# The first mixer's value, gate and memory-query columns computed token by token, with its heads turned between output units

## The reference

```python
proj = rms_norm(x, mix_norm_g) @ a_w_in       # q, k (4 heads x 128), v, o (4 x 256), gates (8), xq (4 x 128)
h = num / maximum(abs(den), exp(-m_t))        # num = (q k' * decay) v, den = row sums of the weights
h = rms_norm(h, h_norm_g) * sigmoid(o)        # norm over a head's 256 columns
p = softmax(rms_norm(xq, q_norm_g) @ mem_k' * 128 ** -0.5)
x = x + concatenate([h, p @ mem_v]) @ a_w_out
```

## Time and profile before

| | us |
|---|---|
| median of 3 runs | 1548.07 |
| lowest and highest run | 1547.05, 2189.37 |
| the profiled execution, whole | 1546.74 |
| its span, first to last instruction | 1544.8 |
| PE busy | 1534.3 |
| DVE, ACT, POOL busy | 967.8, 813.4, 220.7 |
| mixer A, from its first matmul to its last output unit | about 215 to 345 |

### The profile page before, as it was taken

How to read it: one execution, slowest core, us unless ns; L and a number is a source line. 1 busy time by engine, 2 the same in 40 slices (tenths; PEclk the granted TensorE clock), 3 DMA queues, 4 the chain that set the end, 5 groups by cost and what they waited for, 6 DMA issues and landing times.

```text
span 1544.8 us, 20354 instructions
## 1 busy us (share of the span) xinstructions
PE 1534.3 (99%) x8114; PEld 1312.3 (85%) x8114; DVE 967.8 (63%) x1108; ACT 813.4 (53%) x1003; POOL 220.7 (14%) x220
## 2 busy tenths in 40 slices
PE   9999999999999999999999999999999999999998
PEld 7888888988888888888888888899988899888886
DVE  6655566666555565556776555589998566665555
ACT  7544454565444454445776444466887343454444
POOL 0211100011111021110001211100571000021110
PEclk9999999999999999999999999999999999999999
DMA  7776666445866567656425776656554665557662
GB/s 250 253 218 204 193 190 211 137 155 172 229 209 213 179 204 222 216 182 196 144 75 168 242 210 206 195 189 201 187 180 151 214 191 191 170 180 224 211 216 89
DMA packets 261679, 296.04 MB, mean 192 GB/s; under 512 B 63812, under 2 KB 223840, under 8 KB 261600
## 3 DMA queue, kind: packets, MB, share of 16 engines
q1 hardware_dynamic: 260496, 293.64, 61.0%
q10 hardware_dynamic: 1104, 1.31, 0.2%
HBM read 280.71 MB, written 1.09 MB: 182 GB/s over the span
## 4 chain that ended last, share of the span: by engine, by line
PE 96%; issue 1%; POOL 1%; DMA 0%; DVE 0%; ACT 0%; ACTq 0%; POOLq 0%; DVEq 0%
PE ps L2137 25%; PE ps L2141 25%; PE ps L2138 25%; PE ps L2127 5%; PE ps L2128 4%; PE ps L2129 4%; PE ps L2180 1%; PE ps L2291 1%; DMA scr<-in_mem_dram 0%; PE ps L2422 0%; PE ps L2405 0%; POOL scr L662 0%; PE ps L2700 0%; PE ps L2602 0%; PE ps L2575 0%
## 5 line engine op out<-in xcount | busy, mean ns | idle before, releaser
L1266 DVE TENSOR_TENSOR w_lo<-w_raw,w_hi 128x2048 fp32r<-128x2048 f32 x255 | 591.8, 2323 | 368.0 <-ACT w_hi L719 367.9
L719 ACT ACTIVATE w_hi<-w_raw 128x2048 fp32r<-128x2048 f32 x255 | 487.3, 1913 | 379.8 <-PE ps L2141 332.2
L2137 PE MATMUL ps<-w_hi,xg_hi 128*128 128x512 f32 (+1 forms) x1072 | 417.9, 390 | 0.0
L2141 PE MATMUL ps<-w_hi,xg_lo 128*128 128x512 f32 (+1 forms) x1072 | 415.6, 388 | 0.0
L2138 PE MATMUL ps<-w_lo,xg_hi 128*128 128x512 f32 (+1 forms) x1072 | 415.5, 388 | 0.0
L2137 PE MATMUL ps<-w_hi,y_hi 128*128 128x512 f32 x666 | 261.9, 393 | 0.8 <-DVE w_lo L1285 0.5
L2141 PE MATMUL ps<-w_hi,y_lo 128*128 128x512 f32 x666 | 259.1, 389 | 0.0
L2138 PE MATMUL ps<-w_lo,y_hi 128*128 128x512 f32 x666 | 258.9, 389 | 0.0
L2137 PEld LDWEIGHTS ps<-w_hi,xg_hi 128*128 128x128 f32 x1072 | 201.3, 188 | 41.5 <-issue 0.7
L2141 PEld LDWEIGHTS ps<-w_hi,xg_lo 128*128 128x128 f32 x1072 | 201.3, 188 | 41.4
L2138 PEld LDWEIGHTS ps<-w_lo,xg_hi 128*128 128x128 f32 x1072 | 201.3, 188 | 40.8
(11 more groups left out here) (339 smaller groups left out, 1148.7 us busy)
## 6 DMA issues: line engine op xcount, KB each, us to landing
w_raw<-in_ffn_w_in_dram SPq DMA_DIRECT2D x176, 512.0 KB, 4.8
w_raw<-in_ffn_w_out_dram SPq DMA_DIRECT2D x88, 512.0 KB, 4.4
w_raw<-in_w_in_dram SPq DMA_DIRECT2D x82, 512.0 KB, 4.7
w_raw<-in_a_w_in_dram SPq DMA_DIRECT2D x28, 512.0 KB, 4.6
w_raw<-in_w_gate_dram SPq DMA_DIRECT2D x22, 512.0 KB, 4.0
w_raw<-in_w_up_dram SPq DMA_DIRECT2D x22, 512.0 KB, 5.0
w_raw<-in_w_down_dram SPq DMA_DIRECT2D x22, 512.0 KB, 4.1
w_raw<-in_w_ssd_proj_dram SPq DMA_DIRECT2D x16, 512.0 KB, 4.7
```

The lines of the kernel that those rows point to most:

```text
L719: act.activation(w_hi[:, u % RING, :], w_raw[:, u % RING, :], ACT.Copy).then_inc(w_rounded, 1)
L1266: dve.tensor_tensor(w_lo[:, s, :], w_raw[:, s, :], w_hi[:, s, :].bitcast(F32), ALU.subtract).then_inc(w_split, 1)
L2137: pe.matmul(dst, xh, hi, start=start, stop=False, skip_group_check=True)
L2141: return pe.matmul(dst, xl, hi, start=False, stop=stop, skip_group_check=True)
```

## The change

All units of mixer A from u+5 on become row units, in the order memory query (u+5, u+6), values (u+7 to u+10), output gate (u+11 to u+14). The memory query is turned by 8 transposes on PE (`memory_query_turn`); its squares are summed by DVE instead of PE. `den` becomes a column per token (12 matmuls of one column and two small transposes), and the heads' sum of squares is taken by ACT with an accumulator while it reads the numerator from PSUM. The gated heads lie by token and are turned to channels by PE, 8 transposes at a time (`head_turn`), once between output units v and v+1 and once between v+1 and v+2. ACT's `high_` then reads these turned heads from PSUM. The output units take the memory part first (v, v+1), then the heads (v+2 to v+5). One of two round trips of rows through memory goes away, and so do POOL's four `tensor_scalar` instructions on the gate.

```diff
-    add("mixa", "ggggg" + "dddd" + "g" * 6)
...
+        GA = [4 + (U["mixa"] + k) % RING for k in range(3)]
+        MA = min(GA[2], GA[0])
+        PAIRS = ((GA[1], STAT), (GA[2], GA[0]))
...
+                sp.wait_ge(vec_done, vec.at("A -m"))
+                sp.dma_start(a_spread, a_rows[0:4, GM]).then_inc(a_stored, 16)
+                sp.wait_ge(a_stored, 16)
+                sp.dma_start(a_nm, a_spread.partition_broadcast(P)).then_inc(nm_landed, 16)
                 for j in range(6):
-                    load(U["mixa_out"] + j, d_src(a["a_w_out"][0], 256 * j))
+                    load(u + 9 + j, row_src(w, 512 * (j % 2), D + 512 + 512 * (j // 2)))
+                for j, k in enumerate((4, 5, 0, 1, 2, 3)):
+                    load(U["mixa_out"] + j, d_src(a["a_w_out"][0], 256 * k))
...
+                for tt in range(2):
+                    act.wait_ge(w_used, u + 7)
+                    act.activation(xq_arows[:, tt], ps[:, PAIRS[1][tt], :], ACT.Identity, scale=rcol[:, tt:tt + 1]).then_inc(act_done, act_(f"A xr {tt}"))
+                for tt in range(2):
+                    act.wait_ge(act_done, act_.at(f"A xr {tt}"))
+                    act.activation(xsq_arows[:, tt], xq_arows[:, tt], ACT.Square).then_inc(act_done, act_(f"A xsq {tt}"))
+                round_(u + 9)
+                for j in range(2):
+                    act.wait_ge(pe_done, pe_.at("A xT"))
+                    act.activation(xq_a[:, 2 * j:2 * j + 2], tiles(ps[:, PAIRS[1][j], :]), ACT.Identity,
+                                   scale=gain_qk[:, 0:1]).then_inc(act_done, act_(f"A xq {j}"))
+                root(m_r, m_v, load=False)
+                round_(u + 10)
...
                                        scale=rcol[:, tt:tt + 1]).then_inc(act_done, act_(f"A v {g} {tt}"))
-                round_(u + 8)
-                round_(u + 9)
                 value_columns(0)
-                round_(u + 10)
                 round_(u + 11)
+                mem_exps("A", p_a)
+                round_(u + 12)
                 value_columns(1)
-                round_(u + 12)
-                act.wait_ge(pe_done, pe_.at("A num 3"))
+                round_(u + 13)
+                mem_turned("A", pt_a, 0)
...
-                    act.wait_ge(vec_done, vec.at(f"A h {h}"))
-                    act.activation(a_hsq[:, 2 * h:2 * h + 2], a_h[:, 2 * h:2 * h + 2],
-                                   ACT.Square).then_inc(act_done, act_(f"A hsq {h}"))
-                round_(u + 13)
-                query_squares("A", u + 9, xq_a, xsq_a, 0)
-                root(KB(28, 4), KB(24, 4))
-                round_(u + 14)
-                root(m_r, m_v, load=False)
+                    act.wait_ge(pe_done, pe_.at(f"A num {h}"))
+                    for tt in range(2):
+                        c = 2 * h + tt
+                        act.activation(a_squares[:, c], half(h, tt), ACT.Square, scale=a_rd[:, c:c + 1],
+                                       accum_out=a_sum[:, c:c + 1]).then_inc(act_done, act_(f"A hsq {c}"))
+                root(a_y2, a_v2, load=False)
                 act.preload_act_table_set(SETS["exp"])
-                def tanh(j):
-                    evacuated(u + 11 + j)
-                    act.activation(a_o[:, 2 * j:2 * j + 2], a_o[:, 2 * j:2 * j + 2], ACT.Tanh,
-                                   scale=0.5).then_inc(act_done, act_(f"A tanh {j}"))
-                def high(j):
-                    act.wait_ge(vec_done, vec.at(f"A y {j}"))
-                    act.activation(y_hi[:, 2 * j:2 * j + 2], a_h[:, 2 * j:2 * j + 2], ACT.Copy).then_inc(act_done, act_(f"A hi {j}"))
+                def tanh(g):
+                    for tt in range(2):
...
+                        act.wait_ge(w_used, u + 13 + 2 * g)
+                        act.activation(a_o[:, tt, 512 * g:512 * g + 512], ps[:, PAIRS[g][tt], :], ACT.Tanh,
+                                       scale=r_half[:, tt:tt + 1]).then_inc(act_done, act_(f"A tanh {g} {tt}"))
+                def high_(g):
+                    act.wait_ge(pe_done, pe_.at(f"A yT {g}"))
+                    for k in range(4 * g, 4 * g + 4):
+                        act.activation(y_hi[:, k], half(PAIRS[g][k % 4 // 2], k), ACT.Identity,
+                                       scale=col("h_norm", k)).then_inc(act_done, act_(f"A hi {k}"))
                 tanh(0)
-                round_(u + 15)
-                high(0)
+                round_(v)
+                high_(0)
+                round_(v + 1)
                 tanh(1)
-                mem_exps("A", p_a)
-                high(1)
-                round_(u + 16)
-                tanh(2)
-                high(2)
                 round_(v + 2)
-                tanh(3)
-                mem_turned("A", pt_a, 4)
-                high(3)
-                round_(v + 3)
-                mem_high("A", 4)
-                for j in range(4, 7):
+                high_(1)
+                for j in range(3, 7):
                     round_(v + j)
...
+                for tt in range(2):
+                    dve.wait_ge(act_done, act_.at(f"A xsq {tt}"))
+                    dve.tensor_reduce(xq_sum.rearrange("p (h t) -> p t h", t=2)[:, tt], xsq_arows[:, tt].rearrange("p (h d) -> p h d", d=M_HD),
+                                      AXX, ALU.add).then_inc(vec_done, vec(f"A xsum {tt}"))
...
                 dve.wait_ge(vec_done, vec.at("A den"))
-                dve.reciprocal(g[:, GL], g[:, GL]).then_inc(vec_done, vec("A rden"))
+                dve.reciprocal(a_rd, a_rd).then_inc(vec_done, vec("A rden"))
+                split(u + 9)
...
+                mem_max("A")
                 split(u + 11)
...
                 gated(0)
-                evac(a_o[:, 2:4], u + 12)
-                split(u + 15)
-                low_a(0)
+                split(v)
+                low_(0)
+                split(v + 1)
                 gated(1)
-                mem_probs("A", p_a)
-                low_a(1)
-                evac(a_o[:, 4:6], u + 13)
-                evac(a_o[:, 6:8], u + 14)
-                split(u + 16)
-                gated(2)
-                low_a(2)
                 split(v + 2)
-                gated(3)
-                low_a(3)
-                split(v + 3)
-                mem_low("A", 4)
-                for j in range(4, 7):
+                low_(1)
+                for j in range(3, 7):
                     split(v + j)
...
-            def row_unit(u, banks, X, kt0, start, stop):
+            def row_unit(u, banks, X, kt0, start, stop, between=None):
...
                     tok = slice(tt * P, tt * P + P)
                     for k in range(4):
                         last = row_passes(ps[:, banks[tt], :], X[0][:, kt0 + k, tok], X[1][:, kt0 + k, tok], s, 512 * k, start and k == 0, stop and k == 3)
...
-                def value_unit(j):
+                g = a_rows[0:4]
+                def rows_of(j, banks, **kw):
+                    row_unit(u + j, banks, (xg_hi, xg_lo), 4 * ((j - 5) % 2), j % 2 == 1, j % 2 == 0, **kw)
+                def gate_columns(row, bank_, c0):
+                    for tt in range(2):
+                        last = pe.transpose(ps[:, bank_, c0 + 4 * tt:c0 + 4 * tt + 4], g[:, row, tt * P:tt * P + P], ident[0:4, 0:4])
+                    return last
+                def scores():
+                    evacuated(u + 4)
+                    for h in range(4):
+                        pe.matmul(ps[:, h, 0:T], a_k[:, h, 0:P], a_q[:, h], start=True, stop=True)
+                        pe.matmul(ps[:, h, T:384], a_k[:, h, P:], a_q[:, h, P:], start=True,
+                                  stop=True).then_inc(pe_done, pe_(f"A s {h}"))
+                def blocks(h):
+                    return ((0, a_s[:, h, 0:P], 0, True, True), (1, a_s[:, h, P:T], 0, True, False), (1, a_s[:, h, T:], 1, False, True))
+                def den():
+                    pe.wait_ge(vec_done, vec.at("A s 3"))
+                    for h in range(4):
+                        for tt, weights, _, first, end in blocks(h):
+                            pe.matmul(ps[:, 0, 2 * h + tt:2 * h + tt + 1], weights, ones[:, 0:1], start=first, stop=end, skip_group_check=True)
+                    pe.wait_ge(act_done, act_.at("A em"))
+                    gate_columns(GE, 0, 8).then_inc(pe_done, pe_("A den"))
+                def memory_query_turn():
+                    pe.wait_ge(act_done, act_.at("A xr 1"))
+                    for h in range(4):
+                        for tt in range(2):
+                            last = pe.transpose(half(PAIRS[1][h // 2], h)[:, tt * P:tt * P + P], xq_arows[:, tt, h * P:h * P + P], ident[:, :])
+                    last.then_inc(pe_done, pe_("A xT"))
+                def num():
+                    pe.wait_ge(act_done, act_.at("A v 1 1"))
+                    for h in range(4):
+                        for tt, weights, block_, first, end in blocks(h):
```

(79 more changed lines are left out.)

154 lines of the change are left out of this document (57 added, 97 removed).

## The result

The kernel after takes 1552.92 us (median of six runs, 1552.30 to 1554.12), the kernel before 1546.94 us beside it (median of six). The ratio is 1.0039, with a 95% interval from 1.0029 to 1.0049: slower by 4.5 to 7.6 us, within 2%. The profiled execution of after took 1552.74 us, its span is 1551.0 us.

What follows compares the result with a forecast made beforehand. PE was taken to bound the kernel, its matmuls' pace plus any added wait. Terms -2.4 + 5.9 + 0.45 + 2.3 = +6.2 us on the profiled 1546.7 gave 1552.9, stated as 1553.0 us; range 1549.5 to 1557.0.

Steps and rivals of the forecast that it cites:

- What bounds the kernel: Whole kernel: time is PE's matmuls at their issue pace plus any added wait; savings on DVE, ACT or POOL worth nothing.
- PE's own work: Mixer A: matmuls and transposes removed, added and changed in layout sum to -2.4 us.
- The six units: Mixer A: six units change to row layout, 5.45 us each instead of 5.75, -1.8 us.
- The two groups of sums: Mixer A: the heads' sums (L2473, 1.54 us) and the query's sums (L2398, 1.70 us) on PE both go.
- The 24 transposes: Mixer A: 8 transposes of the query and 16 of the heads are added, +2.5 us.
- The wait at v+1: Output unit v+1: PE idles while ACT rounds turned heads, then v+1, and DVE splits it, 5.9 us.
- The wait at v+3: Output unit v+3, after the second turn: PE needs it 5.45 us later, the chain takes 5.9, +0.45 us.
- The clock behind the wait: Unit v+1: clock falls within the wait, restart at 1.2 GHz, half of a 4.5 to 5 us ramp lost, +2.3 us.
- Its two ends: Clock evidence from the kernel's ends: 4.5 to 5 us at half pace at the start, fall from 4.1 us of idleness on.
- The rival in which the clock holds: Output units: the clock stays full through the single wait, giving 1550.7 us; chance 22%.
- The rival with a slow unit v+1 throughout: Mixer A: longer ramp or a second late unit, 3 us more than forecast, 1556 us; chance 17%.
- The rival on the other side: Unit v+1: rounding and split done when `head_turn(0)` ends, wait hidden, only PE's saving left, 1544.3 us; chance 4%.

Runs made afterwards that it cites:

- the spread kernel: Kernel after with head halves one output unit later in ACT's and DVE's lists and `den`'s matmuls spread through unit u+8: 1543.84 us, ratio 0.998 to the kernel before.
- the run with both orders: Kernel after with rounding and split of v+1 and v+3 moved ahead of the heads' steps on ACT and DVE: 1545.48 us, ratio 0.9989 to the kernel before.
- the filled wait: Kernel after with six matmuls against zeros added behind the first turn of heads: 1552.82 us, ratio 1.0047 to the kernel before.
- `den` spread alone: Kernel after with only `den`'s one-column matmuls spread through unit u+8, ACT's and DVE's lists unchanged: 1553.53 us.
- ACT's order alone: Kernel after with ACT's roundings of v+1 and v+3 moved ahead of the head roundings, DVE's list unchanged: 1551.55 us, ratio 1.0029 to the kernel before.

## Why the prediction was right, and where only its sum was

**What bounds the kernel**: right. PE's chain, and what stops it, decide; DVE's 14 us of saved work and POOL's 5 us came to nothing.

**PE's own work**, -2.4 predicted: -2.8 in the profile after, -2.7 bare in the spread kernel. The six units gave 2.2 us instead of 1.8. The two groups of sums (-1.54, -1.70) went as said. The 24 transposes cost 2.45 us, the two small ones 0.2. `den` cost 2.67 us against 2.69 of the old one, and two things that the prediction took at nothing, the numerator and the memory output, gave -0.17 and +0.19.

**The wait at v+1**, +5.9 predicted: right in mechanism and in size, and the order of the lists is shown to be its cause by the run with both orders. Its steps in the profile after: four head roundings from 325.69 to 327.13 (1.44; predicted 1.43), the rounding until 329.06 (1.93; 1.90), the split from 329.09 to 331.38 (2.29; 2.29). The two 5.9 are not quite the same length: the prediction counts from the moment at which PE could start the unit, 0.25 us ahead of the transposes' end, and by that count the trace has 6.1. The 0.15 us from the split's end to PE's start were left out. What the prediction didn't see is that DVE's list holds the same obstacle 1 us shorter. It said that `low_(0)` lies under the rounding and costs nothing there, which was true of the kernel as it is, and would have misled whoever mended ACT's list alone.

**The wait at v+3**, +0.45: 0.42 us idle, 0.7 by starts, because the last record ahead of the break lasts 0.16 us beyond the moment at which the next could have started, and the first matmul behind it takes 0.31 us instead of 0.23 (345.44 to 345.75).

**The clock behind the wait**, +2.3: it fell, as said, and not by a fixed amount. In the five profiles with a wait of 4.9 or 5.9 us the part behind the restart is 3.1, 3.3, 5.1, 5.5 and 5.9 us; half of that, 1.5 to 2.9 us, is lost, on average 2.3. So the term is a good mean and a bad forecast of one execution. Its two ends were read too long, though. At the start of the kernel before, the clock record is at its full level from 6.11 us, 4.0 us after the first transpose and not 4.5 to 5, and half of that is 2.0. And the fall, which the prediction placed from 4.1 us of idleness on, came 2.1 us after the transposes' end in the profile after (325.66 to 327.80). The rival in which the clock holds (22%) is refuted for this wait in all five, and the filled wait, one profile, shows what it would have been worth. The rival with a slow unit v+1 throughout was half met in the last of them (`den` spread alone), where 13 of its 24 matmuls ran at half pace.

**The page of the Trainium skill that the prediction cites**, "TensorE: Matmul & The Clock Gate", Part 1, is borne out here as to idle time: the clock fell within every wait of 4.9 or 5.9 us. The dip is a fall without idle time. The page also gives the distance of starts at either level for 512 columns, 426.7 and 215.7 ns. The trace agrees on the first (332.10 to 332.52 and on, 0.43 us); on the second the units here measure 227 ns, and the measurement decides.

**What the prediction missed**: the dip near 263 us, 1.6 us in the first profile. It looked for idle stretches as the only way to lose the clock. `den` was costed by its duration, and as to its duration it was an even trade for the old one; that it streams one column at a time where the old one streamed 128 and 256, which is likely what brings the dip, was passed over.

**The rival on the other side** (wait hidden, 1544.3): its price was right, its condition (ACT passing its waiting instruction) wasn't needed. Once the lists let it happen, the kernels measured 1544.62 and 1543.84 us.

## What to carry to other kernels

When work that waits for PE is written into the list of an engine that also prepares PE's next input, the whole chain from that wait to the input becomes PE's idle time, however early the input's data was there. Look for the same obstacle in every list along the chain (here ACT's and DVE's) before moving it in one, and move it behind as many preparations as there are free buffers: one preparation ahead of it left a wait of 0.7 us here, two left none. An exact sum is no proof of its terms: compare them one by one, and profile a second execution before a term of one or two microseconds is given a cause.

## What the runs showed of the hardware

PE's clock fell while PE was busy without a gap. In the profile after, PE ran these groups and then the first matmuls of a unit:

```profile
259.01 1.03 PE L2440 MATMUL ps<-ident,scr 128*128 128x128 f32 x8
259.88 2.74 PE L2431 MATMUL ps<-ones,scr 128*128 128x1 f32 x24
262.55 0.28 PE L2411 MATMUL ps<-ident,scr 4*128 4x4 f32 x2
262.76 0.66 PE L2117 MATMUL ps<-w_hi,xg_hi 128*128 128x512 f32 x1
263.22 0.63 PE L2118 MATMUL ps<-w_lo,xg_hi 128*128 128x512 f32 x1
263.64 0.63 PE L2121 MATMUL ps<-w_hi,xg_lo 128*128 128x512 f32 x1
```

Behind 24 records of one column, the 512-column matmuls start 0.43 us apart (263.22, 263.64), and the clock record is at its low level from 262.95. The old `den`, 2.69 us of fp32 matmuls of 256 and 128 columns, left the clock at 1.00 in both profiles of before. In one execution (ACT's order alone) the stretch lasted 6.8 us and cost 3 us. That a block of such matmuls brings the fall is likely and not shown.

Where the clock falls within a wait is not fixed: in five executions the fall came 2.4 to 5.2 us after the last transpose had started, and each time the low level then lasted 6.8 us. The later it falls, the more of the low stretch lies behind the wait, where it slows PE's work: 3.1 us of it in the earliest fall, 5.9 in the latest.
